# Attention over pairs of heads: rope parts as rows of their own, and P normalised before its transpose

## The reference, cut to what matters

```python
cq, ckv, kr, gate = split_last(h @ w_in, (384, 256, 32, 1024))
q = (rms_norm(cq, q_norm_g) @ w_uq).reshape(b, n, 16, 64 + 32)
kv = (rms_norm(ckv, kv_norm_g) @ w_ukv).reshape(b, n, 16, 64 + 64)
# q_rope and kr of x (not of c) are rotated: x1 cos - x2 sin, x2 cos + x1 sin
k = concatenate([k_nope, broadcast(kr)]); q = concatenate([q_nope, q_rope])
oc = attention(qc, kc, vc)                       # softmax(q k / sqrt(96)) v
ox = attention(qx, [kc, kx], [vc, vx])
y = (o * silu(gate)) @ w_out
```

## Time and profile before

| | |
|---|---|
| median of 3 runs | 2364.3 us (2363.39 to 2366.1) |
| profiled execution, its own time | 2368.9 us |
| its span | 2367.1 us |
| PE, PEld busy | 87%, 71% of the span |
| DVE, ACT, POOL busy | 48%, 35%, 29% |
| granted clock, mean | 0.928 of 2.4 GHz |

### The profile page before, as it was taken

How to read it: one execution, slowest core, us unless ns; L and a number is a source line. 1 busy time by engine, 2 the same in 40 slices (tenths; PEclk the granted TensorE clock), 3 DMA queues, 4 the chain that set the end, 5 groups by cost and what they waited for, 6 DMA issues and landing times.

```text
span 2367.1 us, 27756 instructions
## 1 busy us (share of the span) xinstructions
PE 2066.5 (87%) x10852; PEld 1683.4 (71%) x10852; DVE 1143.4 (48%) x1717; ACT 819.1 (35%) x1113; POOL 689.7 (29%) x304
## 2 busy tenths in 40 slices
PE   4899999999969789778484879999979997999997
PEld 3787878778858677667273658788758875878875
DVE  3331666666457577576699243313332524331332
ACT  3253232332233444543331243324332324332332
POOL 1121000000312232232135424444333542444442
PEclk9799999999979799889697989999989998999998
DMA  7111111111111101112120213332222321322321
GB/s 277 36 54 45 63 54 63 55 63 63 63 47 39 33 28 45 36 29 92 34 69 18 80 63 98 89 98 90 89 80 81 99 89 57 103 85 92 99 82 52
DMA packets 46545, 167.72 MB, mean 71 GB/s; under 512 B 5424, under 2 KB 5552, under 8 KB 46160
## 3 DMA queue, kind: packets, MB, share of 16 engines
q1 hardware_dynamic: 44496, 159.93, 21.1%
q10 hardware_dynamic: 1920, 6.02, 0.7%
HBM read 163.83 MB, written 2.10 MB: 70 GB/s over the span
## 4 chain that ended last, share of the span: by engine, by line
PE 72%; DVE 20%; ACT 5%; issue 2%; DMA 1%; ACTq 0%; POOL 0%; DVEq 0%
PE ps L430 19%; PE ps L431 19%; PE ps L432 19%; PE ps L527 4%; PE ps L537 3%; DVE ex L1116 2%; PE ps L558 2%; DVE hf L1116 2%; DVE acc L1116 2%; DVE sq L1116 2%; DVE Alo L1116 1%; DVE hf L1122 1%; ACT sq L792 1%; DVE tmp L1116 1%; PE ps L464 1%
## 5 line engine op out<-in xcount | busy, mean ns | idle before, releaser
L1100 POOL TENSOR_TENSOR wlo<-raw,whi 128x1024 fp32r<-128x1024 f32 x253 | 616.5, 2449 | 1550.2 <-ACT whi L775 1550.2
L430 PE MATMUL ps<-Ahi,whi 128*128 128x512 f32 (+1 forms) x1328 | 529.8, 399 | 43.9 <-issue 23.5
L431 PE MATMUL ps<-Alo,whi 128*128 128x512 f32 (+1 forms) x1328 | 522.8, 394 | 0.0
L432 PE MATMUL ps<-Ahi,wlo 128*128 128x512 f32 (+1 forms) x1328 | 517.0, 389 | 0.0
L775 ACT ACTIVATE whi<-raw 128x1024 fp32r<-128x1024 f32 x253 | 259.9, 1055 | 701.2 <-PE ps L432 680.2
L430 PEld LDWEIGHTS ps<-Ahi,whi 128*128 128x128 f32 x1328 | 257.6, 194 | 121.8 <-issue 38.9
L432 PEld LDWEIGHTS ps<-Ahi,wlo 128*128 128x128 f32 x1328 | 257.3, 194 | 54.1
L431 PEld LDWEIGHTS ps<-Alo,whi 128*128 128x128 f32 x1328 | 258.3, 194 | 47.8 <-issue 0.2
L1122 DVE SCALAR_TENSOR_TENSOR cv<-ps,vec,cv 128x511 f32<-128x511 f32 (+1 forms) x176 | 131.9, 750 | 320.6 <-ACT cv L792 315.9
L430 PE MATMUL ps<-Fhi,whi 128*128 128x512 f32 x416 | 167.3, 402 | 12.9 <-DVE Flo L1116 12.8
L431 PE MATMUL ps<-Flo,whi 128*128 128x512 f32 x416 | 165.5, 398 | 0.0
(11 more groups left out here) (231 smaller groups left out, 3227.3 us busy)
## 6 DMA issues: line engine op xcount, KB each, us to landing
raw<-in_units SPq DMA_DIRECT2D x301, 512.0 KB, 3.6
X<-in_xT ACTq DMA_DIRECT2D x1, 2048.0 KB, 12.8
out_xT<-X SPq DMA_DIRECT2D x8, 256.0 KB, 2.0
CX<-in_ctxT ACTq DMA_DIRECT2D x1, 1024.0 KB, 15.1
masks<-in_masks ACTq DMA_DIRECT2D x1, 512.0 KB, 3.5
gmw<-in_gmw ACTq DMA_DIRECT2D x1, 384.0 KB, 2.8
bs<-in_bs ACTq DMA_DIRECT2D x1, 384.0 KB, 3.8
vec<-in_vec ACTq DMA_DIRECT2D x1, 312.5 KB, 4.5
```

Of the source, the lines that this page charges most:

```text
L430: nc.tensor.matmul(out, sh, mh, start=first, stop=False)
L431: nc.tensor.matmul(out, sh, ml, start=False, stop=False)
L432: return nc.tensor.matmul(out, sl, mh, start=False, stop=last)
L1100: nc.gpsimd.tensor_tensor(wlo[:, s % CONV, :], raw[:, plan.unit_at[("split", s)] % RAW, :], whi[:, s % CONV, :].bitcast(fp32), ALU.subtrac ...
```

## The change

Units go over pairs of heads: for a pair, each query tile is done for head 2p and then for head 2p + 1. (1) The K projection makes nope of both heads in one tile of 128 rows; ACT copies and scales the even half, DVE (`k_odd`) the odd half. (2) Q has 128 rows: nope 64, rope x cos 32, swapped rope x sin 32 (order reversed for the odd head), made by one DVE multiply with a table of N columns that holds 1 and 0 for context tokens; K holds the rotated kr twice, under both. The table is loaded into `acc` after the gate, and the kr tile comes behind the gate tiles; DVE makes kr in 14 steps after the norms. Q of the first two heads and K of the first pair come ahead of V. (3) DVE makes 1/sum right after the exponential and ACT scales P in place (`normalise`), ahead of the next exponential; P has three buffers (in `sq`) instead of two. (4) The output of a pair and query tile is one PSUM tile: V (64 columns) is stationary, P^T (128 columns) moves, the two heads write partitions 0 to 63 and 64 to 127. It comes out transposed; DVE multiplies it into the gate. ACT makes its high part (`pair_high`) and POOL its low part (`pair_low`) per pair. (5) The transposes, multiplies and splits after the loop are gone; `l0` reads Ohi and Olo and waits for each k tile by itself. (6) PSUM tiles of the loop have fixed buffers: scores 0 and 1, transposes 3 and 2, outputs 2, projections 3. (7) In the attention ACT's weight copies may come 24 tiles ahead. The modulation's rows go to `rstd` instead of `hf`. The PE loop below stands for the plan, ACT's and DVE's loops, which have the same places for Q, K and modulation.

```diff
-SPLITS = [("n0", 8), ("cq", 3), ("ckv", 2), ("attn", 8), ("n1", 8)]
+SPLITS = [("n0", 8), ("cq", 3), ("ckv", 2), ("n1", 8)]
...
-UNITS = [(h, q) for h in range(H) for q in range(TN)]
+PAIRS = H // 2
+UNITS = [(2 * p + i, q) for p in range(PAIRS) for q in range(TN) for i in range(2)]
...
+            slot = (slots or range(BANKS2))[self.turn % len(slots or range(BANKS2))]
+            self.turn += 1
+            self.slot.append(slot)
+            self.before.append(self.in_slot.get(slot))
+            self.in_slot[slot] = n
...
+            tile(("S", u), [("p", u + 1)], slots=[u % 2])
+        def out(p, q):
+            tile(("O", p, q), [("og", TN * p + q + 1)], slots=[2])
...
+            tile(("PT", u), [(("pta", "ptb")[i], u // 2 + 1)], slots=[3 - i])
...
+            queries0(0)
+            queries0(1)
+            keys0(0)
...
             def score(u):
                 h, q = UNITS[u]
+                p, i = divmod(h, 2)
                 ps = tile(("S", u))
                 if q == 0:
                     pe.wait_ge(sem("q_nope"), h + 1)
-                    pe.wait_ge(sem("q_rope"), 4 * h + 4)
-                    pe.wait_ge(sem("k_nope"), h + 1)
-                    pe.wait_ge(sem("kr"), 6)
+                    pe.wait_ge(sem("q_rope"), h + 1)
+                    pe.wait_ge(sem(("k_even", "k_odd")[i]), p + 1)
+                    pe.wait_ge(sem("kr"), 14)
                 for c0, c1 in (BOTH if q < TX else [(T, N)]):
                     o0 = c0 if q < TX else 0
-                    last = nc.tensor.matmul(ps[:, o0:o0 + c1 - c0], Q[0:96, h % 2, q * P:(q + 1) * P],
-                                            K[0:96, h % 2, c0:c1], start=True, stop=True)
+                    last = nc.tensor.matmul(ps[:, o0:o0 + c1 - c0], Q[:, p % 2, i, q * P:(q + 1) * P],
+                                            K[:, p % 2, i, c0:c1], start=True, stop=True)
                 done(last)
 
-            def out(u):
-                h, q = UNITS[u]
-                ps = tile(("O", u))
-                pe.wait_ge(sem("pt"), u + 1)
+            def out(p, q):
+                ps = tile(("O", p, q))
+                pe.wait_ge(sem("pta"), TN * p + q + 1)
+                pe.wait_ge(sem("ptb"), TN * p + q + 1)
                 keys = unit_keys(q)
-                for i, t in enumerate(keys):
-                    last = nc.tensor.matmul(ps[:, 0:HV], PT[:, u % 2, i * P:(i + 1) * P],
-                                            V[:, t, h * HV:(h + 1) * HV], start=i == 0, stop=i == len(keys) - 1)
+                for n, t in enumerate(keys):
+                    for i in range(2):
+                        h = 2 * p + i
+                        last = nc.tensor.matmul(ps[64 * i:64 * i + 64, 0:P], V[:, t, h * HV:(h + 1) * HV],
+                                                PT[:, i, n * P:(n + 1) * P], start=n == 0, stop=n == len(keys) - 1)
                 done(last)
 
             pe.wait_ge(sem("v"), TN)
             more = [(0, j) for j in range(8, 12)] + [(1, j) for j in range(12)]
-            qk(0)
             score(0)
             score(1)
             for u in range(NU):
-                if u % TN == 1 and u // TN + 1 < H:
-                    qk(u // TN + 1)
-                if u % TN == 3:
-                    ada(*more[u // TN])
-                if u % TN == 5:
-                    ada_t(*more[u // TN])
+                p, q, i = u // (2 * TN), u // 2 % TN, u % 2
                 if u + 2 < NU:
                     score(u + 2)
+                if i == 0 and u:
+                    out(*divmod(u // 2 - 1, TN))
                 ps = tile(("PT", u))
-                pe.wait_ge(sem("p"), u + 1)
-                for i in range(len(unit_keys(UNITS[u][1]))):
-                    last = nc.tensor.transpose(ps[:, i * P:(i + 1) * P], Pr[:, u % 2, i * P:(i + 1) * P], ident[:, :])
+                pe.wait_ge(sem("pn"), u + 1)
+                for n in range(len(unit_keys(q))):
+                    last = nc.tensor.transpose(ps[:, n * P:(n + 1) * P], Pr[:, u % 3, n * P:(n + 1) * P], ident[:, :])
                 done(last)
-                if u:
-                    out(u - 1)
-            out(NU - 1)
+                if i:
+                    if q in (1, 3) and p + 1 < PAIRS:
+                        queries0(2 * p + 2 + q // 2)
+                    if q == 2 and p + 1 < PAIRS:
+                        keys0(p + 1)
+                    if q in (0, 4):
+                        ada(*more[2 * p + q // 4])
+                    if q in (2, 5):
+                        ada_t(*more[2 * p + q // 4])
+            out(PAIRS - 1, TN - 1)
             for m in range(8):
-                ps = tile(("OT", m))
-                pe.wait_ge(sem("o"), NU)
-                for t in range(TN):
-                    last = nc.tensor.transpose(ps[:, t * P:(t + 1) * P], O[:, t, m * P:(m + 1) * P], ident[:, :])
+                ps = tile(("l0", m))
+                for k in range(KD):
+                    pe.wait_ge(sem("ol"), k + 1)
+                    w = tuple(weights(("l0", m), k))
+                    for c0, c1 in BOTH:
+                        last = product(ps[:, c0:c1], w, (Ohi[:, k, c0:c1], Olo[:, k, c0:c1]), k == 0, k == KD - 1)
                 done(last)
-            for m in range(8):
-                tile(("l0", m))
-                done(linear(("l0", m), Ahi, Alo, 0, SAT["attn"] + 1, BOTH))
...
-            ac.dma_start(rope[:, :], a["rope"]).then_inc(sem("consts"), 16)
...
-                    if plan.first_use[s] > n + AHEAD:
+                    attention = plan.index[("S", 0)] <= n < plan.index[("l0", 0)]
+                    if plan.first_use[s] > n + (24 if attention else AHEAD):
...
+            ac.dma_start(acc[:, :], a["rope"]).then_inc(sem("rope"), 16)
+            psum("kr")
+            sc = float(NOPE + ROPE) ** -0.5
+            def queries0(h):
+                ps = psum(("Q", h))
+                r = (slice(0, 64), slice(64, 128))[h % 2]
+                act(Q[r, h // 2 % 2, h % 2, :], ps[r, 0:N], ACT.Copy, sem_name="q_nope")
+            def keys0(p):
+                ps = psum(("K", p))
+                act(K[0:64, p % 2, 0, :], ps[0:64, 0:N], ACT.Copy, None, sc, "k_even")
...
             def softmax(u):
                 n = P * len(unit_keys(UNITS[u][1]))
                 ps = psum(("S", u))
-                if u >= 2:
-                    ac.wait_ge(sem("psum"), plan.index[("PT", u - 2)] + 1)
+                if u >= 3:
+                    ac.wait_ge(sem("psum"), plan.index[("PT", u - 3)] + 1)
                 ac.wait_ge(sem("mx"), u + 1)
-                act(Pr[:, u % 2, 0:n], ps[:, 0:n], ACT.Exp, small[:, 0, u % 8:u % 8 + 1], 1.0, "p",
+                act(Pr[:, u % 3, 0:n], ps[:, 0:n], ACT.Exp, small[:, 0, u % 8:u % 8 + 1], 1.0, "p",
                     small[:, 1, u % 8:u % 8 + 1])
 
-            qk(0)
+            def normalise(u):
+                ac.wait_ge(sem("rc"), u + 1)
+                n = P * len(unit_keys(UNITS[u][1]))
+                act(Pr[:, u % 3, 0:n], Pr[:, u % 3, 0:n], ACT.Copy, None, small[:, 2, u % 8:u % 8 + 1], "pn")
+            def pair_high(p):
+                ac.wait_ge(sem("og"), TN * p + TN)
+                act(Ohi[:, p, :], gate0[:, p, :], ACT.Copy, sem_name="oh")
             softmax(0)
             softmax(1)
+            normalise(0)
             for u in range(NU):
-                if u % TN == 1 and u // TN + 1 < H:
-                    qk(u // TN + 1)
+                p, q, i = u // (2 * TN), u // 2 % TN, u % 2
+                if u + 1 < NU:
+                    normalise(u + 1)
                 if u + 2 < NU:
                     softmax(u + 2)
-            for m in range(8):
-                psum(("OT", m))
-                high(Ahi[:, m, :])
+                if i:
+                    if q in (1, 3) and p + 1 < PAIRS:
+                        queries0(2 * p + 2 + q // 2)
+                    if q == 2 and p + 1 < PAIRS:
+                        keys0(p + 1)
+                    if q == 1 and p:
+                        pair_high(p - 1)
+            pair_high(PAIRS - 1)
...
+            def pair_low(p):
+                po.wait_ge(sem("oh"), p + 1)
+                nc.gpsimd.tensor_tensor(Olo[:, p, :], gate0[:, p, :], Ohi[:, p, :].bitcast(fp32),
+                                        ALU.subtract).then_inc(sem("ol"), 1)
+            def before_split(n):
+                while lowered[0] < PAIRS and n >= plan.index[("PT", 12 * lowered[0] + 16) if lowered[0] < PAIRS - 1 else ("O", PAIRS - 1, TN - 1)]:
+                    pair_low(lowered[0])
+                    lowered[0] += 1
...
+            ROWS = [(slice(64, 96), slice(96, 128)), (slice(32, 64), slice(0, 32))]
+            sc = float(NOPE + ROPE) ** -0.5
+            ps = psum("kr")
+            ve.wait_ge(sem("rope"), 16)
+            for i, (r, r2) in enumerate(ROWS):
+                k = K[r, 0, i, :]
+                tt(k, ps[r, 0:N], acc[r, :], MUL, "kr")
```

(95 more changed lines are left out.)

112 lines of the change are left out of this document (50 added, 62 removed).

## The result

| | before | changed |
|---|---|---|
| median | 2364.6 us | 2298.1 us (2295.9 to 2300.1, 4 runs) |
| ratio, 95% interval | | 0.9718 (0.9701 to 0.9735) |
| profiled execution, its own time | 2368.9 | 2295.9 |
| span | 2367.1 | 2294.2 |

Faster by 66.5 us in the medians, where 84.3 were forecast (2280 us, a ratio of 0.964). The time lies in the range of 2262 to 2314.

What follows compares the result with a forecast made beforehand. PE bounds the kernel; 36.8 us of work plus 1.0 of waits per pair give a 298.6 us loop, l0 starts 82.0 us sooner, 84.9 with the clock: 2280 us, range 2262 to 2314.

Steps and rivals of the forecast that it cites:

- What bounds the kernel: Whole kernel: PE, busy 87% of the span, sets the time; a second off its instruction stream is a second saved.
- 24.9 and 27 us of work in 37.8: Attention loop, per pair: softmax chain 24.9 us and DVE's own work 27, both under the pair's 37.8.
- Part 1, keys: K projection: two heads' k_nope share one product, 2.1 us less per pair.
- Part 2, outputs: Attention outputs: two column halves side by side, full output 1.40 us with tiling changes, short 0.58; 5.2 us less per pair.
- rival (c): Outputs: no packing, a 64-column pass costs 0.107 us; 42 us more, 2322 us; chance 0.08.
- Rival (d): Outputs: alternating column halves costs 0.27 us a change, 448 changes, 121 us; 2401 us, slower; chance 0.03.
- rival (b): Outputs: each tiling change empties the array, 0.27 us both ways, 96 changes, 26 us instead of 6; 2300 us; chance 0.06.
- all waits stay: Attention loop: if all 2.6 us of PE waits per pair remain, the time is 2293 us.
- 1.0 us per pair for waits: Attention loop: allowance for weight and high copies ahead of an exponential, added to 36.8 us of PE work per pair.
- Part 3, P early: Softmax: P normalised before its transposes, 2.39 us per full unit, stays under PE; third buffer lets exponentials pass late transposes.
- Part 4, rope: Before the loop: kr steps beside Q0, Q1, K0 and V products, 0.7 us wait allowed; first scores at 223.9, no gain.
- Part 5, the end: After the loop: transposes, multiplies and splits go; l0 starts at 523.0 instead of 605.04, full clock saves 2.9 us more.

Runs made afterwards that it cites:

- k_twice: Changed kernel with each pair's K products made twice into the same tile; ratio 0.9762 to before, median 2310.1 us.
- rc_twice: Changed kernel with each of the 96 reciprocals made twice, 0.20 us more per unit; ratio 0.9731 to before, 2303.7 us.
- mod_first: Changed kernel with query tile 2's transposed modulation step in buffer 2 (not in the last pair), read by DVE ahead of K; ratio 0.9682 to before, 2290.2 us.
- ahead7: Changed kernel with weight copies in the attention at most 7 tiles ahead instead of 24; ratio 0.9753 to before, 2306.9 us.

## Why the prediction was right, and where it was off

**What bounds the kernel, and that it stays PE:** right for the steady pairs. k_twice puts all of 2.1 us into each pair, rc_twice a quarter of what it adds to the chain. It was nearer, though, than "24.9 and 27 us of work in 37.8" sounds (DVE's terms as written add up to about 26, and 26.47 was measured): with the order on ACT turned round, PE meets it at once. In the last pair, without Q and K, outputs waited 3.5 us for copies that follow this chain.

**Part 1, keys:** 2.1 us per pair, confirmed.

**Part 2, outputs:** two passes side by side, right. A full output took 1.46 us, or 1.60 with the changes around it, where I took 1.40 for both together; 37 us come back without the halves, where rival (c) had 42. That choice rested on 32-column rows only; 64 columns behave alike. Rival (d), that alternating costs, is the reverse of what happens: the alternation is what makes two halves run side by side. The changes of tiling were undersized: I read them as free on the way in. They are 0.09 in and 0.05 out, and the output itself had 0.17 over the 1.29 of twelve passes: 0.31 instead of my 0.11, so 0.2 us too little per full output. A short one took 0.59 and 0.14 around it where I had 0.58. Together that is 0.8 + 0.3 = 1.1 us per pair, 9 in the kernel. The Trainium skill, TensorEngine Tiling (Array Packing), Key Properties, has changes of mode draining TensorE; what shows around the output is 0.14 us for the two changes, about a quarter of the 0.54 that rival (b) gave them, so the measurement does not bear out a full emptying of the array at each change. The Trainium skill, TensorEngine Tiling (Array Packing), Overview, puts two column tiles at up to twice the speed. The runs agree with it: 2.68 / 1.46 is 1.84, and 1.68 with the 0.14 for the changes.

**What the total does not tell.** The median of 2298.1 lies nearer to rival (b)'s 2300 than to the forecast's 2280, and near the 2293 for "all waits stay". It confirms neither: a change of tiling took 0.14 for both ways and not 0.54, and no transposes waited for P in a steady pair.

**The step that failed is the 1.0 us per pair for waits.** I had it for weight and high copies ahead of an exponential; in the steady pairs of the trace PE never waits for those. I played P, the row maxima and the reciprocals through, but not the PSUM buffers of the projections. K, the transposed step and Q share buffer 3. At query tile 2 the step comes right behind K, so PE stands until ACT and DVE have emptied K: 1.17 us, with 0.26 behind it, mostly DVE's longer half. mod_first took 1.4 us off each pair by moving it, and brought the pair to 38.04. That this is near the forecast's 37.8 is partly luck, as what is left over 36.8 is not the wait that I counted but the tiling. Over the 36.8 us of counted work a pair took 2.65: 1.4 here, 1.1 in the outputs and their changes of tiling, and 0.15 that is the balance of small terms, of which Q's wait for the transposes' copy in the same buffer (0.3, 1.9 us in seven waits) is one. Beside the steady pairs, the last one took 2.4 more than counted, and its outputs waited 3.5 us. Of that about 1 us belongs to the weight copies, for which I had 1.5 (in ahead7, without them, the wait of 1.64 was 0.67 and that of 1.34 stayed). The rest is the softmax chain where no Q and K lie beside it, which I had at nothing.

**Part 3, P early:** right in that no P was late in the steady pair. The third buffer, which I gave a role, brings no time.

**Part 4, rope:** no gain at the start, as worked out; PE waited 1.34 us for Q's buffer where 0.7 was allowed. The start of the scores was met within 0.2 us, which is also luck: in the variants, with the same code ahead of it, it lay between 223.5 and 225.5.

**Part 5, the end:** the gap and the half clock are gone as described. The look-ahead was charged with 1.5 us and credited with nothing; ahead7 shows that it carries 8 us, about half of it since the shorter tail would otherwise have brought l0 up against its own weights, the rest in the pairs.

## What to carry to other kernels

When small matmuls are packed into column groups, let the groups alternate within a few passes, keep a packed product in one piece, and count, by the figures of this case, some 0.3 us for each visit from full width and back (1.46 us where 12 passes of 0.107 would be 1.29, and 0.14 around it). When a loop's PSUM buffers are fixed by hand, list for each buffer who empties it and what PE issues next into it: two short steps in a row through one buffer expose the full evacuation. And when a stage in front gets shorter, look at the work that prepares the next stage, since its due times move forward too.

## What was unexpected

In this kernel the halves of the array ran side by side only for passes that lie near one another in PE's order: 2.68 us for 24 passes at full width, 2.39 with one run of 12 per half, 1.51 with runs of 4, 1.46 with runs of 2.
